# Key products of two tiles moved into the preceding stage, and the last memory gate in column pieces, in a two-layer decoder step

## The reference

```python
def shared_kv(h, pos, g, w_kv, k_g):
    k, v = jnp.split(rms_norm(h, g) @ w_kv, [W_DIFF], axis=-1)
    k = rope(rms_norm(k.reshape(bsz, t, DIFF_HEADS, 2, DIFF_HD), k_g), pos)
    ...
def b_layer(...):
    xn = rms_norm(h, norm_g)
    q, mem_q, gate = jnp.split(xn @ w_in, [W_DIFF, W_DIFF + W_MEM], axis=-1)
    ...
    lam = jnp.exp(jnp.sum(lv[0] * lv[1])) - jnp.exp(jnp.sum(lv[2] * lv[3])) + lam_init
    ...
    mo = mem_attend(mem_q, mem_k, mem_v, mq_g).astype(h.dtype)
    y = jnp.concatenate([o, mo], axis=-1) * jax.nn.silu(gate)
```

## Time and profile before

| what | us |
|---|---|
| runs | 2237.68, 2231.25, 2235.39 |
| median | 2235.39 |
| profiled execution, its own time | 2233.48 |
| its span (first to last instruction) | 2231.8 |
| mean granted TensorE clock | 0.978 of full speed |
| busy time: PE, DVE, ACT, POOL | 2102.9, 890.0, 640.5, 318.8 |

### The profile page before, as it was taken

The page is one execution under the profiler, slowest core; times in us unless marked ns, Lnnn a source line. Parts: engine busy times, 40 slices in busy tenths (PEclk is TensorE's granted clock), DMA queues, the critical chain, the costliest instruction groups (busy, mean ns, idle before and its releaser), DMA issues. The chain is left out here.

```text
span 2231.8 us, 46600 instructions
## 1 busy us (share of the span) xinstructions
PE 2102.9 (94%) x20542; PEld 1381.4 (62%) x20542; DVE 890.0 (40%) x1758; ACT 640.5 (29%) x1471; POOL 318.8 (14%) x279
## 2 busy tenths in 40 slices
PE   6999999999999999997998899999989899899997
PEld 3577586595785865964454455555555566566664
DVE  3244363453542634623232230316213388743232
ACT  5232321222223312213123312122223266631111
POOL 0000020020110200202001121211100166410110
PEclk9999999999999999999999999999999999899998
DMA  7010010010100100101602111210020100276762
GB/s 267 17 34 12 11 32 21 11 43 20 31 23 11 32 22 11 42 20 58 242 1 80 57 65 52 94 70 0 10 85 27 52 7 1 76 269 212 238 223 71
DMA packets 53948, 147.80 MB, mean 66 GB/s; under 512 B 11587, under 2 KB 21123, under 8 KB 52468
## 3 DMA queue, kind: packets, MB, share of 16 engines
q1 hardware_dynamic: 43764, 103.97, 13.8%
q0 software_dynamic: 9984, 40.87, 5.3%
HBM read 123.58 MB, written 21.24 MB: 65 GB/s over the span
## 5 line engine op out<-in xcount | busy, mean ns | idle before, releaser
L756 PE MATMUL psum<-xT,rw_w 128*128 128x384 f32 (+1 forms) x1152 | 399.4, 486 | 2.8 <-PEq L169 2.8
L756 PEld LDWEIGHTS psum<-xT,rw_w 128*128 128x128 f32 x1152 | 207.0, 190 | 120.8 <-issue 13.7
L2060 PE MATMUL psum<-spare,xT 128*128 128x384 f32 (+1 forms) x432 | 143.3, 494 | 1.5 <-PEq L169 1.5
L2060 PE MATMUL psum<-kvq_w,xT 128*128 128x384 f32 (+1 forms) x432 | 140.6, 487 | 0.0
L1294 DVE SCALAR_TENSOR_TENSOR rwkv_xs<-psum,rwkv_pc,rwkv_xsc 128x64 f32<-128x64 f32 x90 | 25.5, 284 | 238.6 <-PE psum L973 238.6
L2060 PEld LDWEIGHTS psum<-spare,xT 128*128 128x128 f32 (+1 forms) x432 | 80.4, 187 | 62.7 <-issue 13.6
L2060 PEld LDWEIGHTS psum<-kvq_w,xT 128*128 128x128 f32 (+1 forms) x432 | 79.0, 184 | 61.3 <-issue 11.2
L1103 ACT COPY rwkv_r_sb<-psum 128x64 f32<-128x64 f32 x96 | 20.3, 212 | 325.4 <-PE psum L955 294.2
L724 POOL DMA_DIRECT2D out<-rwkv_s x6 | 5.7, 953 | 755.3 <-ACT rwkv_out_p L1124 755.3
L1536 PE MATMUL psum<-xT,gate_w 128*128 128x384 f32 (+1 forms) x288 | 96.8, 485 | 6.6 <-PEq L169 6.6
L2139 DVE TENSOR_REDUCE kvq_ss<-kvq_sq 128x6 f32<-128x384 f32 (+1 forms) x36 | 19.9, 552 | 201.6 <-ACT kvq_sq L2102 201.4
(11 more groups left out here) (439 smaller groups left out, 3936.9 us busy)
## 6 DMA issues: line engine op xcount, KB each, us to landing
kp<-in_cache_k SPq DMA_DIRECT2D x64, 384.0 KB, 4.1
xT<-in_cache_v POOLq DMA_DIRECT2D x48, 384.0 KB, 4.3
rw_w<-in_w_in SPq DMA_DIRECT2D x28, 512.0 KB, 3.8
gate_w<-in_cache_v POOLq DMA_DIRECT2D x16, 384.0 KB, 5.2
front_w<-in_mem_w_kv SPq DMA_DIRECT2D x2, 2048.0 KB, 14.3
x_rows<-in_x_p SPq DMA_DIRECT2D x8, 512.0 KB, 14.2
h<-in_x_p SPq DMA_DIRECT2D x8, 512.0 KB, 14.0
residual<-h POOLq DMA_DIRECT2D x8, 512.0 KB, 3.4
```

What stands on the lines that cost most here:

```text
L756: mm = pe.matmul(out, w[:, load % 2, k, :], xT[:, k, a:b], start=(k == 0), stop=(k == KC - 1))
L2060: mm = pe.matmul(bank[0:r, j % 6, 0:W], xT[:, k, n * P:n * P + r], w[i % 2][:, k, :], start=(k == 0), stop=(k == KC - 1))
```

## The change

It does three things.

- The key products of tiles 2 and 3 (first half of the keys) are made in `out0`, into banks 2 and 3, where `kvq` would put them: those of tile 2 behind the products of tile 7 and ahead of the transposes of tiles 5 and 6, those of tile 3 behind these transposes and ahead of the transposes of tile 7. They wait for the weights' gain, for both copies of their tile and for the sixteenth add, which frees the banks. In `kvq` the first group leaves the two tiles out, and the products of tile 1 raise `mm_done` by three.
- The last job of `MemoryQueries` (g1) signals after each of its three column ranges. ScalarE does the two exponentials without waiting for it, and then a Tanh for each range; VectorE makes the gate range by range.
- VectorE's three steps for lambda and the gains go ahead of that last job.

```diff
@@ class MemoryQueries
+    LAST = len(JOBS) - 1
...
             for k in range(KC):
                 mm = pe.matmul(out[:, a:b], self.w[n][:, k, :], self.xT[:, k, a:b], start=(k == 0), stop=(k == KC - 1))
-        mm.then_inc(self.ready, 1)
+            if m == self.LAST:
+                mm.then_inc(self.ready, 1)
+        if m < self.LAST:
+            mm.then_inc(self.ready, 1)
...
-        act.wait_ge(self.ready, m + 1)
+        if m < self.LAST:
+            act.wait_ge(self.ready, m + 1)
...
             act.wait_ge(self.s_read, 2)
             for cc in range(2):
                 nc.scalar.activation(sq[:, cc, :], sq[:, cc, :], ACT.Exp, scale=-0.5).then_inc(self.rn_ready, 1)
+            for j, (a, b) in enumerate(COLS):
+                act.wait_ge(self.ready, m + 1 + j)
+                b = min(b, TT)
+                nc.scalar.activation(self.gates[c][:, a:b], self.psum(m)[:, a:b], ACT.Tanh, scale=0.5).then_inc(self.tanh_ready, 1)
+            return
...
+                for j, (a, b) in enumerate(COLS):
+                    dve.wait_ge(self.tanh_ready, c + 1 + j)
+                    b = min(b, TT)
+                    g = self.gates[c][:, a:b]
+                    nc.vector.scalar_tensor_tensor(out=g, in0=g, scalar=1.0, in1=self.psum(m)[:, a:b], op0=ALU.add,
+                                                   op1=ALU.mult).then_inc(self.g_read, 1)
+                return
@@ last_sums_and_norm
+AHEAD = (2, 3)
...
-            nc.gpsimd.tensor_tensor(next_w, next_w, bcast(next_gain.unsqueeze(2), [P, KC, 384]), ALU.mult)
+            nc.gpsimd.tensor_tensor(next_w, next_w, bcast(next_gain.unsqueeze(2), [P, KC, 384]), ALU.mult).then_inc(next_gained, 1)
...
+            def next_products(n):
+                pe.wait_ge(next_gained, 1)
+                pe.wait_ge(act_out, AT[n] + 1)
+                pe.wait_ge(dve_out, AT[n] + 1)
+                pe.wait_ge(added, 2 * NTILE - 2)
+                for k in range(KC):
+                    pe.matmul(bank[:, n, 0:384], xT[:, k, n * P:(n + 1) * P], next_w[:, k, :], start=(k == 0), stop=(k == KC - 1))
+
             products(GROUPED[0])
             for g in range(1, len(GROUPED)):
                 products(GROUPED[g])
+                if g == len(GROUPED) - 1:
+                    next_products(AHEAD[0])
                 turns(GROUPED[g - 1])
+            next_products(AHEAD[1])
             turns(GROUPED[-1])
@@ keys_values_queries
+                    if i == 0 and n in AHEAD:
+                        continue
                     for k in range(KC):
                         mm = pe.matmul(bank[0:r, j % 6, 0:W], xT[:, k, n * P:n * P + r], w[i % 2][:, k, :],
                                        start=(k == 0), stop=(k == KC - 1))
-                    mm.then_inc(mm_done, 1)
+                    mm.then_inc(mm_done, 1 + len(AHEAD) if i == 0 and n + 1 == AHEAD[0] else 1)
...
-            for m in range(6):
+            for m in range(5):
                 mem.dve(dve, m)
             dve.wait_ge(exp_ready, 1)
...
+            mem.dve(dve, 5)
```

More of the change, by code:

```diff
@@ L1850, in last_sums_and_norm @@
         rstd = st.sb("rstd", [P, NTILE])
-        cleared, unit_mm, added, rstd_ready, xn_ready, turned, act_out, dve_out, next_loaded, act_chain, stored = st.sems(
-            "cleared unit_mm added rstd_ready xn_ready turned act_out dve_out next_loaded act_chain stored")
+        cleared, unit_mm, added, rstd_ready, xn_ready, turned, act_out, dve_out, next_loaded, next_gained, act_chain, stored = st.sems(
+            "cleared unit_mm added rstd_ready xn_ready turned act_out dve_out next_loaded next_gained act_chain stored")
         block = st.block()
```

## The result

The changed kernel took 2220.6 us (median of five runs, 2218.2 to 2223.7), against 2235.39 us before: ratio 0.994, 95% interval 0.9928 to 0.9951. That is 14.8 us less by the medians, where 14.6 was forecast (2220.8 us); the ratio, which goes by the means, gives 13.4 us less, with an interval of 11.0 to 16.1.

A forecast was written before the change was run, and what follows sets the result against it. TensorE was taken as the bound, busy for 94% of the 2231.8 us span. Terms 4.0 + 2.8 + 4.9 + 2.9 = 14.6 us, off the median 2235.39, gave 2220.8 us; range 2216.7 to 2228.0.

The forecast's parts named there:

- Tiles 2 and 3 in `out0`: End of `out0`: `kvq` starts 6.3 us later, its key group has 10.32 us less to do; gain 4.0 us.
- The clock at `kvq`'s start: First tile of `kvq`: starts at full clock instead of 0.50; gain 2.8 us, bounds 0 and 2.8.
- the sum of 8.9 us: Both stage starts: neither clock term counted on, only the other two; as rival "both stay cold" 2226.5 us, chance 0.11.
- The last gate: End of `kvq`: roots and small steps earlier, gate in pieces, so TensorE starts `mem1` 4.9 us earlier.
- The clock at `mem1`'s start: First piece of `mem1`: full clock kept over 1.7 to 2.1 us idle; gain 2.9 us, bounds 0 and 2.9.
- The rival of one cold start: Between `kvq` and `mem1`: about 2 us idle lowers the clock, last term lost; 2223.7 us, chance 0.20.
- The four terms: `out0`, `kvq` and `mem1`: two tiles' work 4.0, `kvq` clock 2.8, last gate 4.9, `mem1` clock 2.9; sum 14.6 us.
- the rival of the accident: Stage starts, posed in the experiments: the clock is an accident of the execution, not of work ahead; no chance given.
- The slower rival: Transposes from 1236 to 1241 in `out0`: clock falls and dense work doesn't restore it; about 2271 us, chance 0.02.

The follow-up runs named there:

- The kernel that makes them twice: Changed kernel, but `kvq` makes the products of tiles 2 and 3 again, over those from `out0`; 2230.56 us against 2232.87 for the kernel before.
- the gate in one piece: Changed kernel, but the last gate's Tanh and gate step are one piece each of 1088 columns; 2223.76 us against 2232.87 for the kernel before.
- one tile: Changed kernel, but only tile 2's products are made in `out0`, tile 3's back in `kvq`; 2223.56 us against 2234.70 for the kernel before.
- the tail alone: Changed kernel without the products in `out0` and the skipping of tiles; last gate as changed; 2224.12 us against 2232.87 for the kernel before.
- the first three tiles: Changed kernel with three tiles' products in `out0`, first group reordered 2, 3, 0, 1, 4 to 8; 2217.74 us against 2234.70 before, run again 2216.50.
- the fourth: Kernel with three tiles ahead, plus tile 3's products directly behind tile 2's in `out0`; 2217.31 us, beside 2216.50 for three tiles.

## Why the prediction was right

*Tiles 2 and 3 in `out0`.* Forecast 6.3 us later, measured 5.99. No wait was late. The 16 transposes took 1.75 us to the next product instead of 1.97, and the way from the last 8 to `kvq`'s first product 2.55 instead of 2.6. The key group is two tiles shorter: from `kvq`'s first product to the second group's first it takes 49.50 us before and 36.43 with the change, so 13.07 less, of which 2.75 is the clock of the next term and 10.32 the two tiles, as worked out. The kernel that makes them twice has 10.38 us more in the stage (356.16 less 345.78).

*The clock at `kvq`'s start.* Forecast 2.8 us, measured 8.25 - 5.50 = 2.75. Of this term the size is sure only for the pair of executions: the start that follows bare transposes cost 8.25 us in one and 7.20 in another execution of the same code. The start took 5.50 us in all eight profiles in which products stood directly ahead of the last transposes and the wait behind these was 1.51 us. The Trainium skill (TensorE: Matmul & The Clock Gate, What's actually happening) warns that the number of slow matmuls differs between executions. The traces agree for the start behind bare transposes (8.25 and 7.20 us); the start behind dense work and a wait of 1.51 us was not slow in any of the eight, so the sum of 8.9 us, which counted on neither start, did not come.

*The last gate.* Forecast 4.9 us, measured 4.80 (21.43 less 16.63). The last pieces took the 0.41 us that was forecast and 0.45 for 0.46; the barrier took about 0.9 us, between the two values that were weighed.

*The clock at `mem1`'s start.* Forecast 2.9 us, measured 2.90. The first piece took 5.43 or 5.44 us in all nine profiles with 1.84 us of idle time, and 8.17 to 8.33 in the three with 3.35 or 6.64. The rival of one cold start had the right mechanism, as the gate in one piece shows with 3.35 us; the wait of 1.84 us was short enough. The rows at hand spoke for either (1.68 us of idle time that kept the clock, 2.8 that lost part of it), so this term was weighed, with 0.31 against it, and not worked out.

*What the forecast left out.* The four terms make 14.8 us in the traces, the same as the medians moved, but the span of the profiled execution moved by 12.9, and the means of the runs by 13.4, as did the medians when the changed kernel was run again. That the medians came within 0.2 us of the forecast is luck. The profiled execution lost 3.0 us ahead of tile 7's products, where TensorE's instructions are the same: 1.7 up to the start of `out0`, and 1.3 in the stretch at 0.52 that the table of stretches above shows, in which 16 products took 8.86 us instead of 7.57. The trace before has a shorter stretch at 0.50 there (1225 to 1228). From the start of `out0` to these products it took 42.40 us in the trace before and with one tile, and 43.3 to 43.9 with the changed kernel, run twice, and five others that have the same instructions there. There is one trace of the kernel before, so no run shows whether the change makes the longer stretch more frequent. The execution lost 0.6 us more behind `mem1`'s first piece, where the twelve profiles differ by 4.5, and gained 1.7 within `kvq`.

This gain is of the clock too, at a place of which the forecast says nothing. `kvq` transposes its queries in two runs of instructions (line 2048, with the change 2079), each behind products and a wait. The second run and the products behind it, before and with the change:

```profile
1588.19 0.93 PE L2048 MATMUL psum<-base,kvq_rot 128*128 128x128 f32 x6 [2.23 <-ACT QT L2083]
...
1592.41 17.02 PE L1372 MATMUL psum<-xT,y_m 128*128 128x292 f32 x48
1609.27 1.99 PE L1369 MATMUL psum<-kvq_mq_sq,base 128*128 128x292 f32 x6
```

```profile
1585.04 0.93 PE L2079 MATMUL psum<-base,kvq_rot 128*128 128x128 f32 x6 [2.24 <-ACT QT L2116]
...
1588.71 14.89 PE L1373 MATMUL psum<-xT,y_m 128*128 128x292 f32 x48
1603.44 1.99 PE L1370 MATMUL psum<-kvq_mq_sq,base 128*128 128x292 f32 x6
```

From the first of these rows to the last, the same instructions behind the same wait took 21.08 us before (granted clock 0.53 over 1592 to 1597) and 18.40 with the change (1.00 over 1589 to 1597), 2.7 less; at the first run the change lost 0.9 (20.23 instead of 19.29). The second place took 18.4 us in the six profiles with two tiles ahead and 19.1 to 21.1 in the other six; with one tile it was 21.11, and 0.5 less than in the changed kernel at the first run, which is where that kernel's 2.2 us went. The kernel that makes the products twice and the tail alone have the same instructions in `kvq` and took 18.40 and 19.14. What decides the clock at this place no run shows, and the rival of the accident isn't excluded there. The slower rival, a clock that dense work doesn't bring back, showed nowhere.

## What to carry to other kernels

Work that is moved from a busy stage into an earlier one gives what it fills there of the engine's idle time, and what it does to the clock at the next start; here the first three tiles filled waits, and the fourth, which had none to fill, came 5.16 us later in one stage and 5.0 us shorter in the next. A short wait ahead of dense matmuls can cost more afterwards than it lasts: 1.5 us of extra work behind the last product cost 2.8 us more at half clock in the next stage. So the work behind a stage's last product is worth cutting into pieces even where nothing but the last piece is on the path.

## What the runs showed of the hardware that was not expected

Extra products that are thrown away were not pure cost in the traces: 10.3 us of them cost 6.0 us in `out0`, and the next stage's first tile was then 2.75 us faster than before (1.70 faster than with the tail alone), at a granted clock that held over 1.51 us of idle time. With 3.30 us of idle time behind the same products it didn't hold. The runs' times are too far apart to confirm the gain.

Behind the second transposes of the queries, after the same wait of 2.2 us and the same instructions, TensorE ran at full clock in six profiles and below it in six.
